# Row scaling of two weight matrices moved from GpSimd to ScalarE, with a new order of root and splitting work around it

## The reference

```
y = gmlp(rms_norm_2(h, a_pre_g)) ; its last product is  y @ a_w_out   (2048 x 1024)
h = h + rms_norm_2(y, a_post_g)
kv_in = rms_norm_2(h, kv_norm_g)
k, v  = kv_in @ w_k , kv_in @ w_v                       (1024 x 256 each)
q, z  = split(rms_norm_2(h, b_pre_g) @ b_w_in)          (1024 x 2048)
```

## Time and profile before

| | us |
|---|---|
| median of 3 runs | 901.84 |
| the profiled execution's own time | 902.16 |
| its span (first to last instruction) | 900.4 |
| TensorE busy | 875.2 |
| GpSimd busy | 556.4 |
| VectorE busy | 542.6 |
| ScalarE busy | 356.4 |

### The profile page before, as it was taken

How to read it: one execution, slowest core, us unless ns; L and a number is a source line. 1 busy time by engine, 2 the same in 40 slices (tenths; PEclk the granted TensorE clock), 3 DMA queues, 4 the chain that set the end, 5 groups by cost and what they waited for, 6 DMA issues and landing times.

```text
span 900.4 us, 11943 instructions
## 1 busy us (share of the span) xinstructions
PE 875.2 (97%) x4224; PEld 727.0 (81%) x4224; DVE 542.6 (60%) x878; ACT 356.4 (40%) x792; POOL 556.4 (62%) x620
## 2 busy tenths in 40 slices
PE   8999999999999999999999999999977999999997
PEld 5888888888888777888888888888866988888886
DVE  6125647775035489676766625556975457878624
ACT  5124332431134367545112311123634436766622
POOL 7766556576789832318974058762397798556352
PEclk9999999999999999999999999999998999999999
DMA  7443231332422467895742254327932122211202
GB/s 198 140 129 103 71 91 50 94 140 89 133 83 94 142 129 164 212 219 167 175 126 90 75 165 122 111 94 178 223 115 69 47 95 71 71 48 62 80 1 94
DMA packets 81516, 102.65 MB, mean 114 GB/s; under 512 B 11825, under 2 KB 54321, under 8 KB 81458
## 3 DMA queue, kind: packets, MB, share of 16 engines
q1 hardware_dynamic: 72752, 85.12, 29.5%
q0 software_dynamic: 8704, 16.78, 11.0%
q10 hardware_dynamic: 2, 0.00, 0.0%
HBM read 99.79 MB, written 2.10 MB: 113 GB/s over the span
## 4 chain that ended last, share of the span: by engine, by line
PE 90%; POOL 5%; issue 2%; DVE 1%; ACT 1%; DMA 0%; POOLq 0%; DVEq 0%; ACTq 0%
PE bank L2036 27%; PE bank L2037 27%; PE bank L2038 27%; PE bank L2264 2%; PE bank L2292 1%; PE bank L2120 1%; POOL wlo L843 1%; PE bank L2237 1%; PE bank L2287 1%; PE bank L2286 1%; POOL tok L813 1%; POOL raw L813 1%; DVE tok L1428 1%; POOL v5lo L843 1%; ACT junk L942 1%
## 5 line engine op out<-in xcount | busy, mean ns | idle before, releaser
L843 POOL TENSOR_TENSOR wlo<-raw,whi 128x512 fp32r<-128x512 f32 x204 | 280.8, 1407 | 0.1
L836 POOL TENSOR_SCALAR whi<-raw 128x512 fp32r<-128x512 f32 x202 | 141.8, 738 | 185.4 <-PE bank L2038 176.4
L2036 PE MATMUL bank<-actB_hi,whi 128*128 128x512 f32 (+1 forms) x416 | 159.5, 383 | 2.3 <-POOL wlo L843 2.3
L2037 PE MATMUL bank<-actB_lo,whi 128*128 128x512 f32 (+1 forms) x416 | 158.6, 381 | 0.0
L2038 PE MATMUL bank<-actB_hi,wlo 128*128 128x512 f32 (+1 forms) x416 | 158.5, 381 | 0.0
L2036 PE MATMUL bank<-whi,actA_hi 128*128 128x512 f32 x320 | 128.5, 402 | 6.7 <-DVE wlo L1702 5.0
L2037 PE MATMUL bank<-wlo,actA_hi 128*128 128x512 f32 x320 | 126.2, 394 | 0.0
L2038 PE MATMUL bank<-whi,actA_lo 128*128 128x512 f32 x320 | 126.2, 394 | 0.0
L2036 PEld LDWEIGHTS bank<-actB_hi,whi 128*128 128x128 f32 x416 | 78.2, 188 | 17.5 <-issue 2.9
L2038 PEld LDWEIGHTS bank<-actB_hi,wlo 128*128 128x128 f32 x416 | 78.2, 188 | 15.1
L2037 PEld LDWEIGHTS bank<-actB_lo,whi 128*128 128x128 f32 x416 | 78.3, 188 | 14.1
(11 more groups left out here) (262 smaller groups left out, 1593.7 us busy)
## 6 DMA issues: line engine op xcount, KB each, us to landing
raw<-in_a_w_in SPq DMA_DIRECT2D x44, 512.0 KB, 4.3
raw<-in_w_in SPq DMA_DIRECT2D x32, 512.0 KB, 3.8
raw<-in_b_w_in SPq DMA_DIRECT2D x16, 512.0 KB, 3.4
raw<-in_a_w_out SPq DMA_DIRECT2D x12, 512.0 KB, 3.4
gain<-in_a_w_out POOLq DMA_DIRECT2D x9, 512.0 KB, 8.6
raw<-in_w_out SPq DMA_DIRECT2D x8, 512.0 KB, 4.0
raw<-in_w_ple_gate SPq DMA_DIRECT2D x8, 512.0 KB, 3.3
gain<-in_a_w_in POOLq DMA_DIRECT2D x8, 512.0 KB, 7.7
```

The source lines that it names most:

```text
L836: pool.tensor_scalar(H, src[:, i * HALF:(i + 1) * HALF], 1.0, 1.0, ALU.mult, ALU.mult).then_inc(w_hi, 1)
L843: ins = pool.tensor_tensor(L, src[:, i * HALF:(i + 1) * HALF], H.bitcast(f32), ALU.subtract)
L2036: M(out_, whi_, xhi_, start=start, stop=False)
L2037: M(out_, whi_, xlo_, start=False, stop=False)
```

## The change

It has four parts. ScalarE gets a function `scale_two` that scales a half of v5 or k5 by four 128x256 activations, and GpSimd scales neither any more but waits for `w_scaled`. ScalarE's queue is reordered: `hi_a(13)` goes ahead of `square_a(0, 1)`, `h3_out(1)` ahead of `normed_n(0)`, and `normed_n(1)` ahead of `square_a(2, 0)` and `turned_n(0)`; the four calls of `scale_two` stand between them. GpSimd's roots stand elsewhere: h3 0 behind k5's first high parts, h3 1 between its two rests (a new place, n - 0.25), and h3 2, a 3 and h3 3 behind the whole unit. VectorE does both halves of `lo_a(13)` ahead of `part_gain(0, 1)` and `h3_in(0)`.

```diff
             def scale_half(u, h):
...
-                g = kvg if UNITS[u][0] in ("v5", "k5") else bg
                 for k in range(4):
                     pool.tensor_scalar(src[:, k * 256:(k + 1) * 256], src[:, k * 256:(k + 1) * 256],
-                                       g[:, 4 * h + k:4 * h + k + 1], 1.0, ALU.mult, ALU.mult).then_inc(w_scaled, 1)
+                                       bg[:, 4 * h + k:4 * h + k + 1], 1.0, ALU.mult, ALU.mult).then_inc(w_scaled, 1)
...
-                if s in ("v5", "q5", "z5"):
+                if s in ("v5", "k5"):
+                    scaled[0] += 4
+                elif s in ("q5", "z5"):
                     scale_half(u, n % 2)
-                elif s != "k5":
+                else:
                     pool.wait_ge(landed, value)
...
                 for i in range(2):
+                    for f in after.get(n - 0.25, ()) if i else ():
+                        f()
...
-            k5 = UNIT_NO["k5", 0]
-            after[at("v5", 0, 1)] = [lambda: root("a", 0, D), lambda: scale_half(k5, 0), lambda: root("a", 1, D),
-                                     lambda: scale_half(k5, 1), lambda: root("h3", 0, D)]
-            after[at("k5", 0, 0) - 0.5] = [lambda: root("h3", 1, D)]
+            after[at("v5", 0, 1)] = [lambda: root("a", 0, D), lambda: root("a", 1, D)]
+            after[at("k5", 0, 0) - 0.5] = [lambda: root("h3", 0, D)]
+            after[at("k5", 0, 0) - 0.25] = [lambda: root("h3", 1, D)]
             after[at("k5", 0, 0)] = [lambda: root("a", 2, D)]
-            after[at("k5", 0, 1) - 0.5] = [lambda: root("h3", 2, D), lambda: root("a", 3, D)]
-            after[at("k5", 0, 1)] = [lambda: root("h3", 3, D)]
+            after[at("k5", 0, 1)] = [lambda: root("h3", 2, D), lambda: root("a", 3, D), lambda: root("h3", 3, D)]
...
+            def scale_two(s, h):
+                src, landed, value = raw_of(UNIT_NO[s, 0], h)
+                act.wait_ge(landed, value)
+                act.wait_ge(small_in, 16 * 13)
+                for k in range(4):
+                    w = src[:, k * 256:(k + 1) * 256]
+                    A(w, w, ACT.Copy, scale=kvg[:, 4 * h + k:4 * h + k + 1]).then_inc(w_scaled, 1)
...
             square_a(2, 1)
+            scale_two("v5", 0)
             hi_a(12)
             square_a(3, 1)
+            scale_two("v5", 1)
+            hi_a(13)
             square_a(0, 1)
-            hi_a(13)
             square_a(1, 1)
+            scale_two("k5", 0)
             h3_out(0)
+            h3_out(1)
             normed_n(0)
-            h3_out(1)
+            normed_n(1)
+            scale_two("k5", 1)
             square_a(2, 0)
             turned_n(0)
-            normed_n(1)
             turned_n(1)
...
             for r in range(2):
                 add_kept(5, r, a_out_(r, 1), a_out_(r, 1), (c7_made, 28 + 4 * r + 7))
-                if r == 0:
-                    part_gain(0, 1)
-            lo_a(13, (0,))
+            lo_a(13)
+            part_gain(0, 1)
             h3_in(0)
-            lo_a(13, (1,))
             part_gain(1, 1)
```

## The result

The changed kernel takes 895.09 us (median of 4 runs, 894.47 to 895.51) against 902.03 us of the kernel before measured with it (901.46 to 903.75). The ratio is 0.9917 with a 95% interval of [0.9905, 0.993]: faster by 0.8%, 6.3 to 8.6 us. The forecast was 892.3, the direction and the range (889.2 to 896.8) held, and the gain was 7 us where 9.6 were summed up.

What follows compares the result with a forecast made beforehand. The prediction took GpSimd as the limit around a13, then the chain to v's first block. v's third block 9.6 us earlier took 902.16 to 892.6, less 0.3 for the median: 892.3, range 889.2 to 896.8.

Steps and rivals of the forecast that it cites:

- What bounds the kernel: Around a13: TensorE's waits of 4.7 and 3.2 us, with a lower clock behind them, come from GpSimd's late queue.
- What leaves GpSimd: v5's and k5's scaling: 4.7 and 6.9 us leave GpSimd; four ScalarE copies take 1.7; v5 unit ends near 666.9.
- Unit a13: TensorE's unit a13: the 4.74 us wait goes and the unit ends near 672.9 instead of 681.25, 8.4 us earlier.
- The chain to v's first block: From VectorE's h3_in(0) to rest_n: this becomes the bound; the block starts at 679.8 instead of 686.32, 6.5 us earlier.
- From there to v's third block: v's first two blocks (4.5 and 2.9 us), transposes and k: third block near 694.8 instead of 704.44, 9.6 us earlier.
- After it: From q5 on: GpSimd is 10 us and TensorE 9.6 us earlier, and what follows moves as one block.
- What would show it: Trace signs: L1702 wait gone, clock 1.00 from 665 to 672, longest wait for rest_n or turned_n, v's first block near 679.8.
- (1): At v's first two blocks: the clock stays low and both run at half clock, 4.2 us more, 896.5; chance 0.12.
- (2): VectorE and GpSimd no longer hinder one another; h3_in at 0.75, 1.0 to 1.5 us less, 889.2 to 890.5; chance 0.10.
- (3): The stall moves whole: tiles 0 and 1 hold v's first block until 686, nothing gained, 901.8; chance 0.04.
- (4): v's weights land late, so their scaling on ScalarE delays hi_a(12); slower, 903.8; chance 0.03.

Runs made afterwards that it cites:

- experiment 1: The kernel before with only the two orders around a13 changed (VectorE's lo_a(13), ScalarE's hi_a(13)), all scaling left on GpSimd: 902.38 us, ratio 0.9995.
- experiment 2: The changed kernel with the two orders around a13 undone, scaling on ScalarE and places of the roots kept: 894.82 us, ratio 0.9919 to the kernel before.
- experiment 8: The changed kernel with lo_a(13) as four subtractions of 128x512 instead of two of 128x1024: 894.45 us, ratio 0.9911 to the kernel before.
- experiment 7: The changed kernel with 20, 8 and 24 transposes of a constant in TensorE's idle times up to v's first block: 893.95 us, ratio 0.9908 to the kernel before.
- experiment 4: The changed kernel with square_a(2, 0) ahead of normed_n(1) and k5's second scaling behind turned_n(1) on ScalarE: 894.61 us, ratio 0.9903 to the kernel before.

## Why the prediction was right, and what it mis-sized

**What bounds the kernel.** Held. TensorE's two waits came from GpSimd's queue, and of the change's parts the new orders around a13, which leave that queue alone, brought nothing (experiments 1 and 2).

**What leaves GpSimd.** Held within 0.3 us. The timelines of ScalarE and GpSimd in the changed kernel:

```profile
654.11 1.71 ACT L1299 ACTIVATE raw<-raw,kvg 128x256 f32<-128x256 f32 x4
656.98 2.01 ACT L1144 ACTIVATE whi<-gain 128x1024 fp32r<-128x1024 f32 x2 [1.16 <-PE bank L2049]
...
668.02 1.71 ACT L1299 ACTIVATE tok<-tok,kvg 128x256 f32<-128x256 f32 x4 [2.16 <-DMA tok<-in_w_k]
...
674.69 1.15 ACT L1290 ACTIVATE big<-resid,rstd 128x1024 f32<-128x1024 f32 x1
676.95 1.15 ACT L1290 ACTIVATE big<-resid,rstd 128x1024 f32<-128x1024 f32 x1 [1.11 <-POOL rstd L794]
678.00 1.69 ACT L1299 ACTIVATE tok<-tok,kvg 128x256 f32<-128x256 f32 x4
```

```profile
655.92 1.20 POOL L837 TENSOR_SCALAR v5hi<-raw 128x512 fp32r<-128x512 f32 x2 [9.85 <-ACT raw L1299]
657.10 3.00 POOL L846 TENSOR_TENSOR v5lo<-raw,v5hi 128x512 fp32r<-128x512 f32 x2
...
663.78 3.53 POOL L846 TENSOR_TENSOR v5lo<-raw,v5hi 128x512 fp32r<-128x512 f32 x2
667.41 1.67 POOL L791 TENSOR_SCALAR ms<-ss 128x1 f32<-128x1 f32 x1
669.17 0.57 POOL L794 TENSOR_TENSOR rstd<-ms,mhalf 128x1 f32<-128x1 f32 x1
...
673.39 0.61 POOL L791 TENSOR_SCALAR ms<-ss 128x1 f32<-128x1 f32 x1
...
674.62 1.27 POOL L846 TENSOR_TENSOR wlo<-tok,whi 128x512 fp32r<-128x512 f32 x1
675.97 0.30 POOL L791 TENSOR_SCALAR ms<-ss 128x1 f32<-128x1 f32 x1
```

Four scaled copies took 1.71 us (1.7 forecast), the first of them in the gap ahead of `hi_a(12)`; the v5 unit ended at 663.78 + 3.53 = 667.3 (666.9 forecast, and this trace is 0.3 late at the common point). k's first scaling waited for its weights until 668.02, not 666.5, because VectorE was later with a12 (its rests began at 658.86 instead of 657.74) and SP issued the load at 661.59 instead of 659.61. That I had not foreseen; it cost nothing, since `h3_out(0)` had its data only at 670.56.

**Unit a13.** The end near 672.9 was forecast and 673.1 measured. The prediction's own terms, 4.74 + 3.1 + 0.3, add up to 8.1 us and an end at 673.1, and not to the 8.4 that it states; nothing in the sum of 9.6 hangs on that, since v's first block was priced by the chain. But I booked the 8.4 us there as the source of the gain, of which 6.5 were "left" at v's first block. Experiment 2 shows that a kernel whose a13 still waits is as fast. The number was right and the reading of it misleading: the chain behind root a 0 set v's first block, and a13 is only cover in front of it. In experiment 2 root a 0 ended 1.1 us earlier from the common point, and v's first block came only 0.2 earlier, since the second half of a13's rests (1.21 us) stood again between `h3_in(0)` and `part_gain(1, 1)`.

**The chain to v's first block.** Here the sum went wrong, by 2.3 of the 2.6 us: 25.4 us from the common point instead of 23.2. Two terms:

```profile
664.45 3.94 DVE L1715 TENSOR_TENSOR wlo<-raw,whi 128x1024 fp32r<-128x1024 f32 x2
668.32 0.68 DVE L1867 TENSOR_TENSOR big<-big,gain 128x512 f32<-128x512 f32 x1
669.77 1.42 DVE L1875 SCALAR_TENSOR_TENSOR resid<-big,rstd,resid 128x512 f32<-128x512 f32 x2 [0.77 <-POOL rstd L794]
...
671.90 1.93 DVE L1875 SCALAR_TENSOR_TENSOR resid<-big,rstd,resid 128x512 f32<-128x512 f32 x2
```

(a) "root a 0 near 667.9": it ended at 669.74. Its first instruction, on 128x1, took 1.67 us instead of 0.30, while VectorE ran a13's rests (3.94 us for two, to 668.4) and, straight behind them, `part_gain(0, 1)` (0.68 us, to 669.0). I had priced contention for VectorE's long instructions and none for GpSimd's short ones. VectorE's `h3_in(0)` made up 0.4 of it, at 1.42 where I had 1.8. At the end of `normed_n(0)` the kernel was 1.1 us behind the forecast. Experiment 8 moved this term the right way: the first instruction by 0.5 and the root's end by 0.8 us.

(b) "GpSimd's root h3 1 is ready at 674.2, in time": it was ready at 676.9. ScalarE's squares of tile 1 ended at 674.6, but k5's first rest (674.62, 1.27 us) stood ahead of it in GpSimd's queue, and `normed_n(1)` waited 1.11 us. The change's own new place for this root did that, and the working passed over it. At the end of `normed_n(1)` the kernel was 2.3 us behind the forecast, 1.2 of it by this term.

From `normed_n(1)` to the block, scaling, square, high part and rest, 4.3 us were forecast and 682.42 - 678.10 = 4.3 measured.

**From there to v's third block.** 15.0 us forecast, 15.4 measured. The first two v blocks took 682.42 to 690.39, 8.0 us, against 7.5: 22 of the first block's 24 matmuls came 0.21 us apart, the cost at the clock of 0.50, so that block took 5.1 us where 4.5 had been booked. **After it** the distance held to 0.1 us.

**What would show it.** The wait for L1702 was gone, the clock was 1.00 up to a13's end, and v's first block started at 682.42, ahead of the 683 that would have refuted the forecast but 2.6 later than the 679.8 named. One sign missed: the longest wait was to be one for `rest_n` or `turned_n`; it is still the one for the normalized tile (2.72 us), ahead of the 2.24 for `rest_n(0)`.

**The rivals.** (1), the low clock: present, but as about 1 us (experiment 7) and not 4.2; the second block ran at full clock. Here the Trainium skill's sentence that low is the default and activity releases it ("TensorE: Matmul & The Clock Gate", What's actually happening) agrees with what was seen: the first block started at 0.50, and with transposes in the gap the clock never fell. (2), less contention: `h3_in` at 1.42 to 1.93 was in part cheaper, but the contention of VectorE and GpSimd moved elsewhere and took back more. The Trainium skill's rule of an exclusive lock ("SBUF — State Buffer", Who interferes with whom) fits the 128x1 instructions of 1.67, 1.15 and 1.14 us, each of which ended within 0.2 us after a VectorE instruction (experiment 8); I had used it only in its favourable direction. (3) is excluded by the result; a case like it occurred in experiment 1, without the scaling. (4) did not occur: v's scaling began at 654.11 and ended ahead of 656.98.

## What to carry to other kernels

In these runs a wait removed from the busiest engine was worth only as much as the chain behind it got shorter; to price a reordering, follow the last dependence of the next stage, not the length of the wait. Work taken off a serial engine goes best into another engine's idle time ahead of the chain: the same 1.7 us on ScalarE cost nothing there, and later in the queue it and the square beside it held v's first block up by 2.4 us (experiment 4). In an in-order queue, write down for each short instruction on the chain (here the roots) what stands directly ahead of it, and look at that again after each move.

## What the runs showed of the hardware

A GpSimd instruction on 128x1 that took 0.30 us where VectorE was idle (670.02 to 670.32 in the kernel before) took 1.67 us beside the last 1.0 us of a VectorE subtraction of 128x1024 with both operands in SBUF and a gain multiplication of 128x512 straight behind it, 1.15 beside such a subtraction with nothing behind it, and 1.14 beside subtractions of 128x512. Four GpSimd scalings of 128x256 took 1.85 us in a quiet stretch and up to 4.31 beside such subtractions and multiplications. Transposes of a constant were enough to keep the granted clock at 1.00 through a gap in which it otherwise fell to 0.50; eight transposes take 1.94 us at 1.2 GHz and 1.06 at 2.4.
